# Two gate products of a linear recurrence, as 64 x 64 blocks in four quarters of the array

## The reference, cut to what matters

```python
xc = causal depthwise convolution of x_raw over 4 taps, + conv_b          # width 512
xb = xc.reshape(bsz, seq, LRU_BLOCKS, LRU_BLOCK_W)                        # 8 blocks of 64
r = jax.nn.sigmoid(jnp.einsum('bshi,hij->bshj', xb, wa).reshape(bsz, seq, width) + ba)
i = jax.nn.sigmoid(jnp.einsum('bshi,hij->bshj', xb, wx).reshape(bsz, seq, width) + bx)
log_a = -LRU_C * r * jax.nn.softplus(a_param)
a = jnp.exp(log_a)
b = jnp.sqrt(jnp.maximum(-jnp.expm1(2.0 * log_a), 0.0)) * (i * xc)
h = scan of  h[t] = a[t] * h[t-1] + b[t]
out = h * jax.nn.gelu(gate_raw)
```

## Time and profile before

| what | value |
| --- | --- |
| median of 3 runs | 1286.14 us (1286.01 to 1286.15) |
| the profiled execution's own time | 1286.48 us |
| its span, first to last instruction | 1284.6 us |
| around the span | 1.9 us |
| mean granted clock of TensorE over the span | 0.998 of full speed |
| HBM traffic | 459.22 MB, 357 GB/s over the span |

### The profile page before, as it was taken

How to read it: one execution, slowest core, us unless ns; L and a number is a source line. 1 busy time by engine, 2 the same in 40 slices (tenths; PEclk the granted TensorE clock), 3 DMA queues, 4 the chain that set the end, 5 groups by cost and what they waited for, 6 DMA issues and landing times.

```text
span 1284.6 us, 14907 instructions
## 1 busy us (share of the span) xinstructions
PE 1243.6 (97%) x6126; PEld 644.3 (50%) x6126; DVE 453.1 (35%) x915; ACT 219.6 (17%) x430; POOL 3.5 (0%) x17
## 2 busy tenths in 40 slices
PE   9999999999999999999999999999998999999996
PEld 8888888998873333333333333333323333333332
DVE  5999924456452522121321213212121312122123
ACT  1722124131040110101111010110101010111102
POOL 0000000000000000000000000000000000000000
PEclk9999999999999999999999999999999999999999
DMA  9533344326979999999999999999999999999996
GB/s 378 205 132 141 121 142 161 124 99 232 411 287 407 429 433 428 433 430 433 433 430 434 430 435 431 433 431 434 431 430 435 430 432 429 431 433 425 427 425 260
DMA packets 31196, 459.22 MB, mean 357 GB/s; under 512 B 4752, under 2 KB 5136, under 8 KB 9264
## 3 DMA queue, kind: packets, MB, share of 16 engines
q1 hardware_dynamic: 27296, 453.00, 84.1%
q10 hardware_dynamic: 3856, 5.59, 1.3%
HBM read 457.53 MB, written 1.05 MB: 357 GB/s over the span
## 4 chain that ended last, share of the span: by engine, by line
PE 71%; DMA 19%; DVE 7%; ACT 1%; issue 1%; DVEq 0%; ACTq 0%; SPq 0%
PE banks L1329 19%; DMA store<-in_moe_w 16%; PE banks L906 15%; PE banks L1365 13%; PE banks L920 4%; PE banks L1337 4%; DMA store<-in_w_last 3%; PE banks L1156 2%; PE banks L1181 2%; PE banks L1436 2%; DVE store L2052 2%; PE banks L1245 2%; PE banks L1347 1%; DVE store L2049 1%; DVE store L2046 1%; DVE store L2051 1%
## 5 line engine op out<-in xcount | busy, mean ns | idle before, releaser
L1329 PE MATMUL banks<-store 128*64 128x512 f32 x1536 | 342.6, 595 | 17.6 <-DMA store<-in_moe_w 17.3
L1329 PEld LDWEIGHTS banks<-store 128*64 128x64 f32 x1536 | 109.3, 137 | 233.1 <-issue 206.2
L1365 PE MATMUL banks<-store 128*64 128x512 f32 x952 | 210.8, 595 | 0.0
L906 PE MATMUL banks<-store 128*128 128x256 f32 x896 | 196.7, 380 | 0.0
L906 PEld LDWEIGHTS banks<-store 128*128 128x128 f32 x896 | 169.4, 190 | 26.0 <-issue 3.5
L2046 DVE TENSOR_SCALAR store<-banks 128x512 f32<-128x512 f32 x32 | 22.1, 692 | 430.0 <-PE banks L1337 430.0
L1365 PEld LDWEIGHTS banks<-store 128*64 128x64 f32 x952 | 65.8, 137 | 142.9 <-issue 120.1
L1337 PE MATMUL banks<-store 128*64 128x512 f32 x512 | 116.8, 598 | 0.4 <-DMA store<-in_moe_w 0.4
L2060 DVE COPY store<-banks 64x512 f32<-64x512 f32 x30 | 20.8, 694 | 203.8 <-PE banks L1365 203.8
L786 ACT ACTIVATE store<-store 128x512 f32<-128x512 f32 x28 | 17.6, 630 | 432.1 <-DVE store L2046 432.1
L1337 PEld LDWEIGHTS banks<-store 128*64 128x64 f32 x512 | 34.2, 136 | 70.1 <-issue 67.7
(11 more groups left out here) (380 smaller groups left out, 845.6 us busy)
## 6 DMA issues: line engine op xcount, KB each, us to landing
store<-in_moe_w SPq DMA_DIRECT2D x72, 4096.0 KB, 30.4
store<-in_moe_w SPq DMA_DIRECT2D x38, 2048.0 KB, 15.3
store<-in_w_in SPq DMA_DIRECT2D x30, 1024.0 KB, 4.8
store<-in_moe_w SPq DMA_DIRECT2D x14, 1024.0 KB, 9.3
store<-in_w_branch SPq DMA_DIRECT2D x8, 1024.0 KB, 4.8
store<-in_w_out SPq DMA_DIRECT2D x4, 1024.0 KB, 6.1
store<-in_w_last SPq DMA_DIRECT2D x4, 1024.0 KB, 32.9
store<-in_w_first SPq DMA_DIRECT2D x4, 256.0 KB, 4.5
```

Source lines behind the costliest of these rows:

```text
L906: last = mm(b[:, j * SEQ:(j + 1) * SEQ], w[:, k, j * P:j * P + P], xT[:, k, :], start=k == 0, stop=k == KD - 1)
L1329: last = mm(bank[into[i]][64 * ct:64 * ct + 64, :], xg[:, 2 * c + kk, col:col + CAP], w[:, kk, i * FF + ct * 512:i * FF + ct * 512 + 512], ...
L1365: last = mm(bank[4][64 * dh:64 * dh + 64, :], actT[:, j, 64 * fh:64 * fh + 64], w[j][:, 512 * dh:512 * dh + 512], start=(fh, j) == (0, 0), ...
```

## The change

On TensorE, each gate product of a tile becomes two products of 64 rows and 64 columns. The first gate's two blocks lie in the quarters (0, 0) and (64, 64) of the array. The second gate's lie in (0, 64) and (64, 0): the block whose input is on partitions 0 to 63 writes to partitions 64 to 127, and the other way round. The four products of a tile are thus in four different quarters. The banks change: the first gates of tiles 0 and 1 share bank 3, those of tiles 2 and 3 bank 4, the second gates lie likewise in banks 5 and 6. The semaphore is still raised once per tile, by the last of the four.

On ScalarE, the first gate's sigmoid is as before but for its bank. The second gate's becomes two instructions of 64 partitions each; each reads one partition half of the bank and writes the other half of `lr_i`, which puts the halves back. The wait before tiles 0 and 1 is for two tiles, that before tiles 2 and 3 for four, since two tiles share a bank.

On the host, the columns of `bx` are rolled by 64 partitions, so that the bias lies on the partitions that are read.

```diff
@@ scalar
             for i in range(4):
-                act.wait_ge(S["gate_psum"], i + 1)
-                nc.scalar.activation(lr_r[:, i, :], bank[3 + i][:, 0:SEQ], ACT.Sigmoid, bias=v_("ba", i)).then_inc(S["gate_act"], 1)
-                nc.scalar.activation(lr_i[:, i, :], bank[3 + i][:, SEQ:], ACT.Sigmoid, bias=v_("bx", i)).then_inc(S["gate_act"], 1)
+                act.wait_ge(S["gate_psum"], i // 2 * 2 + 2)
+                lo = i % 2 * SEQ
+                nc.scalar.activation(lr_r[:, i, :], bank[3 + i // 2][:, lo:lo + SEQ], ACT.Sigmoid, bias=v_("ba", i)).then_inc(S["gate_act"], 1)
+                for r in (0, 64):
+                    c = r ^ 64
+                    ins = nc.scalar.activation(lr_i[r:r + 64, i, :], bank[5 + i // 2][c:c + 64, lo:lo + SEQ], ACT.Sigmoid, bias=v_("bx", i)[c:c + 64])
+                ins.then_inc(S["gate_act"], 1)
@@ tensor
                 pe.wait_ge(S["xc_ready"], i + 1)
-                mm(bank[3 + i][:, 0:SEQ], wa[:, i, :], xc[:, i, :], start=True, stop=True)
-                mm(bank[3 + i][:, SEQ:], wx[:, i, :], xc[:, i, :], start=True, stop=True).then_inc(S["gate_psum"], 1)
+                lo = i % 2 * SEQ
+                for w, b, swap in ((wa, 3, 0), (wx, 5, 64)):
+                    for r in (0, 64):
+                        c = r ^ swap
+                        last = mm(bank[b + i // 2][c:c + 64, lo:lo + SEQ], w[r:r + 64, i, r:r + 64], xc[r:r + 64, i, :],
+                                  start=True, stop=True, tile_position=(r, c))
+                last.then_inc(S["gate_psum"], 1)
@@ host
     columns = [inputs[VECTORS[name]].reshape(-1, P).T for name in VR]
+    turned = list(VR).index("bx")
+    columns[turned] = _np.roll(columns[turned], 64, axis=0)
```

## The result

| | median | lowest to highest | runs |
| --- | --- | --- | --- |
| before | 1285.88 us | 1284.63 to 1286.15 | 12 |
| changed | 1288.28 us | 1286.63 to 1289.28 | 12 |

The ratio is 1.0018, with a 95% interval of 1.0011 to 1.0026: slower by 2.4 us, where 1286.2 was forecast with an upper end of 1287.3. That forecast was 0.1 us above 1286.14, the median of three runs of the kernel before; the median of twelve is 1285.88. The profiled execution took 1288.3, with a span of 1286.5.

A forecast was written before the change was run, and what follows sets the result against it. TensorE was taken to bound the kernel up to about 790 us, then alternating with expert-weight transfers; its 1.45 us saving turns into a wait for ScalarE's 1.43 us delay, net +0.05, rounded to +0.1: 1286.2 us, range 1284.9 to 1287.3.

The forecast's parts named there:

- TensorE's part: Gate products in front of lg 0: sixteen on quarters, four together, take 2.0 us, saving about 1.45 us.
- single file: Rival at the gate products: quarters run one after another because row halves share a bank; +3.8 us, 1289.9, 2%.
- pairs: Rival at the gate products: only two quarters run together, saving nothing on TensorE; +0.34 us, 1286.5, 4%.
- The slack of 1.38 us: Before cq 0: it could have started at 50.68 us, when lg 0's evacuation released it, instead of 52.06.
- Four more cost 4 x 0.36 = 1.43 us: ScalarE's gate sigmoids: four additional ones at the old pitch delay the evacuation of lg 0 by 1.43 us.
- The upper bound that I gave, 2.6 us: ScalarE's added sigmoid time if eight halves don't overlap, 0.5 us each, against four at 0.36.
- dear halves: Rival on ScalarE: halves cost up to 0.5 us each since they cross partitions; +1.2 us, 1287.4, 7%.
- I cost it at nothing: TensorE's clock behind the new wait of some 1.5 us before cq 0: stays at the 2.4 GHz level, cost 0.
- VectorE: Keeps its times, the cosine hidden by 1.0 us; lets TensorE come forward at most 1.1 us at drive(2).
- The end: Last expert transfer: a front part x us shorter starts the stream of weights x us earlier, and the end follows.

The follow-up runs named there:

- e2: Kernel before, with only the second gate's sigmoid split into two 64-partition instructions that read and write the same partitions; 1286.72 us, ratio 1.0008.
- e3: Changed kernel with its twelve sigmoids grouped: four full ones, four halves writing partitions 0 to 63, four writing 64 to 127; 1285.87 us, ratio 1.0001.
- e8: Changed kernel plus four 128 x 128 products that nobody reads, between lg 1 and cq 0; 1287.48 us, ratio 1.0013.
- e4: Changed kernel plus ten 128 x 128 products that nobody reads, between lg 1 and cq 0; 1287.40 us, ratio 1.0014.
- e1: Changed kernel with the second gate's sigmoid one 128-partition instruction again, so the exchanged halves are not put back; 1284.81 us, ratio 0.9992.
- e6: e3 with both lg evacuations on ScalarE ahead of the sine and cosine, and the last four Exp behind them; 1284.30 us, ratio 0.9991.
- e5: The changed kernel itself, unaltered, measured once more; 1288.70 us, ratio 1.0023.

## Why the prediction was wrong, by its own steps

- **TensorE's part** was right. 2.0 us forecast, 1.89 measured and 0.10 more in the chunk behind, with quarters of different rows writing the two partition halves of one bank. The rule that row tiles can't access one bank at the same time ("TensorEngine Tiling (Array Packing)" of the Trainium skill, section "Gotcha 1: PSUM Pressure") doesn't hold in this form; by it the stretch would have been near 7 us in single file, and near 3.8 if quarters of different banks had run in pairs. The rivals of single file and of pairs fall.
- **The slack of 1.38 us** was right, and it turns each kernel's delay on ScalarE into its delay on TensorE: 2.84 - 1.38 = 1.46 in the change (measured with the clock kept up, 101.01 - 99.55 = 1.46), 2.29 - 1.38 = 0.91 in e2 (0.98), 1.70 - 1.38 = 0.32 in e3 (0.30).
- **"Four more cost 4 x 0.36 = 1.43 us"** is the step that failed first. The halves cost no more than others of their width, as assumed (e3), but in the order of the change no sigmoid overlaps its predecessor, the old four included: twelve stand at 0.49 where eight stood at 0.36, and ScalarE is 2.84 us late. The upper bound that I gave, 2.6 us, came from eight halves that don't overlap; it left out that the four full sigmoids between them lose their overlap as well. The "dear halves" rival came nearest, at 7%. But it put the price on crossing partitions, and crossing as such is free (e3), while halves that don't cross lose most of the overlap too (e2). It deserved more than 7%: the row that I took the pitch from was of instructions that all begin at the same partition.
- **"I cost it at nothing"**, for the clock, is the step that failed second. It was a term at nothing, with a reason that held for the forecast's own wait only. I compared a wait of 1.5 us with ones of up to 1.8 us and would have been right for that wait: behind 1.52 (e3) and 1.79 us (e8) the clock stays up. But a rival with a longer wait had to carry the price of the clock, and mine had none. The wait was 2.66 us, behind which the clock fell to its lower level in both profiles, for 1.67 us. The row of tenths that I went by, can't show a fall of 3 us. With the clock kept up, e4 and e8 measured 1287.40 and 1287.48, the 1287.4 of the dear halves. In part that is luck: the rival's delay was 1.2 us on 1286.14, the measured one is 1.6 on 1285.8.
- **VectorE** was right only as far as ScalarE was. With 2.84 us in place of 1.43 the cosine is no longer hidden, and VectorE waits 1.01 us for it; the distances show no cost of this. `drive(2)` does limit the saving, by 0.11 us in e1 and 0.16 in e6.
- **The end** was right. It follows the front: over nine kernels the medians moved by -1.6 to +2.8 us where the distances moved by -1.5 to +3.1, in the same order but for kernels within 0.4 us of each other.

## What to carry to other kernels

A shorter stretch on the bounding engine is worth no more than the slack of the next evacuation, unless that evacuation can come earlier too (e6), so work out that slack to a tenth before you add anything to the engine that evacuates; here 1.38 us decided the sign. If an instruction is split by partitions, keep the parts that begin at the same partition together, since the price is at the changes and falls on the neighbours too. And when a wait grows on TensorE, price the clock behind it for each length of wait that your rivals allow; filling the wait with work that nobody reads is a quick way to measure that price.

## What the runs showed of the hardware

- Successive sigmoids of 256 columns on ScalarE start 0.36 us apart when they begin at the same partitions, and 0.47 to 0.50 in every case here where the first partition read or the first one written changes. In the change the order is (read from 0, write from 0), (64, 0), (0, 64), and all three steps are 0.48 to 0.50; in e2 it is (0, 0), (0, 0), (64, 64) with 0.37, 0.47, 0.50; in e3's groups it is 0.36 to 0.37. The number of partitions and the bank don't matter (e2, e1). This reading fits every distance here, but it is not wholly taken apart. The bias always began at the partition that was read, so the two can't be told from each other. A change of the first partition written alone came only together with a step from 64 to 128 partitions. Other first partitions and other functions weren't tried.
- Four quarters of 64 x 64 run together at 1.89 us for sixteen products of 256 columns, also where two of them share a bank and two share their rows. The chunk behind them takes 0.10 us more than behind whole-array products.
- Behind 2.66 us without work TensorE's granted clock was at 0.50 for 3.4 us in both profiles, beginning 0.6 us (the change) and 0.2 us (e5) after work had started again; by the mean clocks two of 23 executions had no such fall. Behind 0.45, 0.74, 1.52 and 1.79 us it stayed at 1.00, in one profile each. Near 1020 us it fell in five of twelve profiles without a wait over 0.53 us.
